# A mixed attention, recurrence and mixture-of-experts kernel: eight instead of six values units behind the recurrence, and the rotation's additions on GpSimd

## The reference, cut to what matters

```
h = rms_norm(x, g_mix);  proj = h @ w_in
q, k, v, q_idx, k_idx, w_idx = split(proj[dsa part])     # 8 heads of 128; 16 index heads of 64
r, d_w, kr, vr, d_a, d_g = split(proj[recurrent part])   # 16 heads of 64
q = rope(rms_norm(q) * q_gain);  k = rope(rms_norm(k) * k_gain)
q_idx = rope(q_idx);  k_idx = rope(k_idx)
rope(x) = [x1 * cos - x2 * sin, x2 * cos + x1 * sin]
iscore = sum over heads of relu(q_idx . k_idx) * w_idx   # the 64 best keys of each query are kept
y_dsa = softmax(q . k * scale, over the kept keys) @ v
y_rwkv = group_norm(recurrence(r, decay, k, v, ...)) ...
x = x + concat(y_dsa, y_rwkv) @ w_out                    # then experts, then the second block
```

## Time and profile before

| | us |
|---|---|
| median of the runs shown (three) | 3061.78 |
| lowest, highest | 3061.53, 3063.14 |
| the profiled execution's own time | 3059.96 |
| its span in the trace | 3058.2 |
| busy: PE, DVE, ACT, POOL | 2963.6, 1918.1, 1533.6, 162.1 |

### The profile page before, as it was taken

The page is one execution under the profiler, slowest core; times in us unless marked ns, Lnnn a source line. Parts: engine busy times, 40 slices in busy tenths (PEclk is TensorE's granted clock), DMA queues, the critical chain, the costliest instruction groups (busy, mean ns, idle before and its releaser), DMA issues.

```text
span 3058.2 us, 53182 instructions
## 1 busy us (share of the span) xinstructions
PE 2963.6 (97%) x22088; PEld 2645.5 (87%) x22088; DVE 1918.1 (63%) x2591; ACT 1533.6 (50%) x2132; POOL 162.1 (5%) x248
## 2 busy tenths in 40 slices
PE   8999999879899999999999999999999999999998
PEld 7888888768688887776999999999989989898996
DVE  6555555774677878877759954445665545455554
ACT  6445444454566666665543347654344434343443
POOL 0000000200000000000075400000000000000000
PEclk9999999989999999999999999999999999999999
DMA  6233233223588888886444444446555555555554
GB/s 235 85 110 111 98 111 103 89 88 124 191 319 332 321 335 318 329 318 260 152 166 154 152 165 165 167 178 218 182 193 193 193 187 186 192 182 190 191 182 150
DMA packets 81952, 582.43 MB, mean 190 GB/s; under 512 B 9024, under 2 KB 9280, under 8 KB 12480
## 3 DMA queue, kind: packets, MB, share of 16 engines
q1 hardware_dynamic: 79056, 566.45, 50.9%
q10 hardware_dynamic: 2672, 12.71, 1.1%
HBM read 574.93 MB, written 4.19 MB: 189 GB/s over the span
## 4 chain that ended last, share of the span: by engine, by line
PE 87%; DVE 9%; ACT 2%; issue 1%; DMA 0%; ACTq 0%; SPq 0%; DVEq 0%
PE PG L806 10%; PE PG L804 10%; PE PG L807 10%; PE PG L831 6%; PE PG L832 6%; PE PG L830 6%; PE PG L862 5%; PE PG L1241 4%; PE PG L1242 4%; PE PG L1243 4%; PE PG L863 3%; PE PG L864 3%; DVE ring_r L706 3%; PE PX L949 2%; PE PX L1293 1%
## 5 line engine op out<-in xcount | busy, mean ns | idle before, releaser
L706 DVE TENSOR_TENSOR ring_r<-ring,work_r 128x1024 fp32r<-128x1024 f32 x492 | 583.7, 1229 | 334.1 <-ACT work_r L699 330.6
L699 ACT ACTIVATE work_r<-ring 128x1024 fp32r<-128x1024 f32 x492 | 493.1, 1052 | 560.7 <-PE PG L807 290.4
L699 ACT ACTIVATE C_r<-ring 128x1024 fp32r<-128x1024 f32 x268 | 269.1, 1052 | 420.6 <-PE PG L807 296.6
L807 PE MATMUL PG<-YT_r,ring_r 128*128 128x256 f32 x1664 | 469.7, 282 | 0.0
L706 DVE TENSOR_TENSOR ring_r<-ring,C_r 128x1024 fp32r<-128x1024 f32 x268 | 319.7, 1234 | 218.3 <-ACT C_r L699 215.0
L807 PE MATMUL PG<-work_r,ring_r 128*128 128x256 f32 x1344 | 374.7, 279 | 0.0
L807 PEld LDWEIGHTS PG<-YT_r,ring_r 128*128 128x128 f32 x1664 | 316.3, 190 | 0.0
L864 PE MATMUL PG<-HT_r,ring_r 128*128 128x256 f32 x960 | 271.1, 282 | 0.0
L807 PEld LDWEIGHTS PG<-work_r,ring_r 128*128 128x128 f32 x1344 | 253.3, 188 | 0.0
L831 PE MATMUL PG<-ring_r,HT_r 128*128 128x512 f32 x624 | 246.6, 395 | 0.0
L804 PE MATMUL PG<-YT_r,C_r 128*128 128x256 f32 x832 | 238.4, 286 | 6.4 <-DVE ring_r L706 6.4
(11 more groups left out here) (649 smaller groups left out, 7138.4 us busy)
## 6 DMA issues: line engine op xcount, KB each, us to landing
ring<-weights SPq DMA_DIRECT2D x472, 1024.0 KB, 4.8
C<-weights SPq DMA_DIRECT2D x32, 1024.0 KB, 4.9
work<-weights SPq DMA_DIRECT2D x32, 1024.0 KB, 4.9
work<-xT SPq DMA_DIRECT2D x4, 512.0 KB, 7.0
XT<-x ACTq DMA_DIRECT2D x1, 2048.0 KB, 8.2
residual<-XT ACTq DMA_DIRECT2D x4, 512.0 KB, 3.0
XT<-residual ACTq DMA_DIRECT2D x1, 2048.0 KB, 12.3
result<-YT SPq DMA_DIRECT2D x8, 256.0 KB, 2.9
```

What stands on the lines that cost most here:

```text
L699: act.activation(w_high(u)[:, c], weights(u)[:, c], ACT.Copy).then_inc(w_hi, 1)
L706: dve.tensor_tensor(w_low(u)[:, c], weights(u)[:, c], w_high(u)[:, c].bitcast(F32), ALU.subtract).then_inc(w_lo, 1)
L807: last = pe.matmul(o, wl, high[:, k, :], start=False, stop=(n == kts - 1), skip_group_check=True)
```

## The change

Two more v tiles (25 and 26) are moved behind the recurrence: `LATE` is 8, the last pair fills with 4 units instead of 6. The late products are placed anew: ten before PE's wait for `out`, one per square, three per rotation step, 21 in the index steps. The wait for the last tile before the rotation (`DSA_TAKEN`) moves on PE behind the squares and on ACT becomes a wait per tile. ACT's and DVE's splits and ACT's `take_v` of the late units are placed anew. In the rotation, the addition of the two parts goes from DVE to POOL: DVE only writes the sine part (four buffers instead of two, signal a_sin), POOL makes the cosine part (two buffers instead of four) and adds. PE's step r waits for the sine part r - 2, no longer for the finished tile.

```diff
-LATE = 6
-DSA_PER_PAIR = [3] * 7 + [6]
+LATE = 8
+DSA_PER_PAIR = [3] * 7 + [4]
-FILL_UNITS = 6
+FILL_UNITS = [6] * 7 + [4]
...
-        ROPE_C, ROPE_S = cube(area(4 * T), 4), cube(area(2 * T), 2)
+        ROPE_C, ROPE_S = cube(area(2 * T), 2), cube(area(4 * T), 4)
...
             def attention():
+                values(0, 10)
                 pe.wait_ge(DR.sem, DR.at(MT - 1, "out"))
-                pe.wait_ge(free_bank(DSA_TAKEN), DSA_TAKEN // BANKS + 1)
                 for n in range(16):
                     ...
-                    values(n, n + 1)
-
+                    values(10 + n, 11 + n)
+
+                pe.wait_ge(free_bank(DSA_TAKEN), DSA_TAKEN // BANKS + 1)
                 for r in range(25):
                     if r >= 9:
                         pe.wait_ge(a_nrm, r - 8)
                     if r >= 2:
-                        pe.wait_ge(a_rope, r - 1)
+                        pe.wait_ge(a_sin, r - 1)
                     ...
-                    values(16 + 2 * r, 18 + 2 * r)
-
-                values(66, 68)
+                    values(26 + 3 * r, 29 + 3 * r)
+
+                values(101, 103)
                 pe.wait_ge(a_rope, 25)
                 ...
-                values(68, 72)
+                values(103, 107)
...
-                    if 72 + n < LATE * KT:
-                        values(72 + n, 73 + n)
+                    if 107 + n < LATE * KT:
+                        values(107 + n, 108 + n)
...  ACT
-                act.wait_ge(free_bank(DSA_TAKEN), DSA_TAKEN // BANKS + 1)
                 for n in range(16):
+                    if n in (1, 8):
+                        half_high(act, 2 * V_UNIT + 4 + n // 8)
+                    u = P1_AT["dsa", 9 + n]
+                    act.wait_ge(free_bank(u), u // BANKS + 1)
                     if n >= 4:
                         act.wait_ge(a_sum, n - 3)
                     act.activation(SQ[:, n % 4, :], DQ[:, 9 + n, :], ACT.Square).then_inc(a_sq, 1)
-                half_high(act, 2 * V_UNIT + 4)
-                half_high(act, 2 * V_UNIT + 5)
+                half_high(act, 2 * V_UNIT + 6)
                 ... (logarithm and exponential)
+                half_high(act, 2 * V_UNIT + 7)
                 take_v(0)
-                for q in range(1, 4):
-                    half_high(act, 2 * (V_UNIT + 2 + q))
-                    half_high(act, 2 * (V_UNIT + 2 + q) + 1)
+                take_v(1)
+                half_high(act, 2 * V_UNIT + 8)
+                for q in range(2, 6):
                     take_v(q)
+                    half_high(act, 2 * V_UNIT + 5 + 2 * q)
+                    if q < 5:
+                        half_high(act, 2 * V_UNIT + 6 + 2 * q)
...  DVE
+                    if n in (3, 10):
+                        half_low(dve, 2 * V_UNIT + 4 + n // 10)
...
-                late = dict(zip((2, 4, 11, 13, 18, 20), range(2 * V_UNIT + 4, HALVES)))
+                late = dict(zip((3, 6, 9, 11, 14, 16, 19, 22), range(2 * V_UNIT + 6, HALVES)))
                 for r in range(25):
                     if r in late:
                         half_low(dve, late[r])
                     if 9 <= r + 1 < 25:
                         normed(r + 1)
                     dve.wait_ge(a_rot, r + 1)
-                    link(dve.tensor_tensor(ROPE_S[:, r % 2, :], PX[:, 2 + r % 2, 0:T],
-                                           con("sin64" if r < 9 else "sin128"), ALU.mult))
-                    dve.wait_ge(a_cos, r + 1)
-                    dve.tensor_tensor(DQ[:, r, :], ROPE_S[:, r % 2, :], ROPE_C[:, r % 4, :], ALU.add) \
-                       .then_inc(a_rope, 1)
+                    if r >= 4:
+                        dve.wait_ge(a_rope, r - 3)
+                    dve.tensor_tensor(ROPE_S[:, r % 4, :], PX[:, 2 + r % 2, 0:T],
+                                      con("sin64" if r < 9 else "sin128"), ALU.mult).then_inc(a_sin, 1)
...  POOL
-            for r in range(25):
-                pool.wait_ge(a_sq, 1) if r < 9 else pool.wait_ge(a_nrm, r - 8)
-                if r >= 4:
-                    pool.wait_ge(a_rope, r - 3)
-                pool.tensor_tensor(ROPE_C[:, r % 4, :], DQ[:, r, :], con("cos64" if r < 9 else "cos128"),
-                                   ALU.mult).then_inc(a_cos, 1)
+            for n in range(26):
+                if n < 25:
+                    pool.wait_ge(a_sq, 1) if n < 9 else pool.wait_ge(a_nrm, n - 8)
+                    if n >= 2:
+                        pool.wait_ge(a_rope, n - 1)
+                    pool.tensor_tensor(ROPE_C[:, n % 2, :], DQ[:, n, :], con("cos64" if n < 9 else "cos128"),
+                                       ALU.mult).then_inc(a_cos, 1)
+                if n >= 1:
+                    r = n - 1
+                    pool.wait_ge(a_cos, r + 1)
+                    pool.wait_ge(a_sin, r + 1)
+                    pool.tensor_tensor(DQ[:, r, :], ROPE_S[:, r % 4, :], ROPE_C[:, r % 2, :], ALU.add) \
+                        .then_inc(a_rope, 1)
```

More of the change, by code:

```diff
@@ L318, in filling @@
                            for r, name in steps])
-        upto += [KT * FILL_UNITS * p + int(KT * FILL_UNITS * n) // int(share[-1]) for n in share]
-    halves = 2 * FILL_UNITS * MT
+        upto += [KT * sum(FILL_UNITS[:p]) + int(KT * FILL_UNITS[p] * n) // int(share[-1]) for n in share]
+    halves = 2 * sum(FILL_UNITS)
     return upto, [next(i for i, n in enumerate(upto) if n >= KT // 2 * (j + 1)) for j in range(halves)]
@@ L420, in build @@
         DR = Steps(sem("rwkv_dve"), DVE_RW)
-        a_sq, a_sum, a_ms, a_rs, a_nrm, a_rot, a_cos, a_rope = (sem("qk_" + n) for n in (
-            "squared", "summed", "mean_square", "inverse_root", "normed", "rotated", "cos_part", "roped"))
+        a_sq, a_sum, a_ms, a_rs, a_nrm, a_rot, a_sin, a_cos, a_rope = (sem("qk_" + n) for n in (
+            "squared", "summed", "mean_square", "inverse_root", "normed", "rotated", "sin_part", "cos_part", "roped"))
         a_vt, a_v, a_is, a_relu, a_acc, a_bias = (sem("idx_" + n) for n in (
@@ L1721, in attention @@
                     act.activation(RL[:, n % 4, 0:keys], PX[:, n % 4, 0:keys], ACT.Relu).then_inc(a_relu, 1)
-                    if n in (12, 31):
-                        take_v(4 + n // 31)
+                    if n in (8, 24):
+                        take_v(6 + n // 24)
                 act.dma_start(XTOK, A["x"]).then_inc(s_xtok, 16)
```

## The result

| us | before | after |
|---|---|---|
| median of one sitting, 18 executions each | 3061.66 | 3066.20 |
| lowest, highest | 3058.37, 3065.88 | 3061.24, 3078.44 |
| the profiled execution's own time | 3059.96 | 3075.25 |

The ratio after to before is 1.0024, 95% interval 1.0015 to 1.0033: slower by a quarter of a per cent. The forecast of 3065.9 is 0.3 us off, but that closeness is partly luck: the 18 times fall in two groups, eleven from 3061.24 to 3068.31 (median 3064.03) and seven from 3075.25 to 3078.44, and the median falls between. The profiled execution is of the upper group. The page's first line and the trace of the profiled execution of after, by stage: the joint, the squares, the rotation, the idle time before the transposes, the transposes, and the index scores (columns as in the earlier trace rows).

What follows compares the result with a forecast made beforehand. PE, busy 97% of the span, was taken to bound the kernel, DVE its rotation. Terms -10.1 + 0.5 + 1.7 + 1.0 + 11.3 + 1.7 - 2.0 gave +4.1 us, median 3065.9 us, range 3059 to 3072 (3052 to 3075 with rivals).

Steps and rivals of the forecast that it cites:

- A: Last recurrence pair: 28 fewer products ahead of the first group norm product, -10.1 us, with +0.5 for uncovered steps.
- B: End of the recurrence: half_low falls ahead of DVE's var and waits for ACT's half_high, +1.7 us.
- C: Sums of squares: waits at splits, with the half-clock stretch kept, +1.0 us; without that stretch -0.7.
- D: Rotation, 25 steps: bound by POOL, with collisions with DVE's two-SBUF-input instructions, 51.1 us against 39.8, +11.3 us.
- E: After the rotation: PE idles near 7 us for POOL's last adds, then half clock, +1.7 us (bounds 0 and +3.4).
- F: Index scores: 21 filled steps instead of 24, each 0.66 us cheaper unfilled, -2.0 us.
- Rival 1: Rotation: PE-bound at 39.7 us, splits falling into POOL's gaps, no E; total -9.0, 3052.8 us; chance 0.16.
- Rival 2: Rotation: DVE becomes the longer line and POOL waits for each sine; total +11.3, 3073.1 us; chance 0.16.
- Rival 3: Last recurrence pair: with less cover it runs at the pace of the chains; 3072 us; chance 0.08, shared with other.

Runs made afterwards that it cites:

- after_again: The changed kernel run once more without an edit; 3064.49 us, ratio 1.0019 to the kernel before, again in two groups.
- var_first: The changed kernel with DVE's half_low of the last recurrence pair kept behind var; 3066.09 us from five executions.
- psum_high: The changed kernel, ACT also copying the high half into PSUM for the rotation's eight splits, DVE subtracting from there; 3077.79 us, ratio 1.0037.
- refill: The changed kernel with nine late products moved from the index steps ahead of PE's wait for the last addition; 3063.38 us, ratio 1.0000.
- pool_best: The changed kernel with refill, var_first and step 6's half_high between ACT's logarithm and exponential; 3062.36 us, ratio 1.0001.

## Why the prediction was right or wrong

By stages, from the common zero, in us against before; the last row stands at the value transposes behind the index scores.

| | forecast | after | after_again |
|---|---|---|---|
| A, last pair | -9.6 | -9.5 | -9.5 |
| B, joint | +1.7 | +1.8 | +1.8 |
| C, squares | +1.0 | +0.5 | +1.8 |
| D, rotation | +11.3 | +9.9 | +9.9 |
| E, clock at the transposes | +1.7 | +1.7 | +1.7 |
| F, index stage | -2.0 | +13.9 | -0.2 |
| sum | +4.1 | +18.3 | +5.5 |

The spans differ from before's by 15.2 and 3.9. What the table leaves is -2.1 and +0.5 ahead of the zero, and -1.0 and -2.1 behind the last row, where half-clock stretches stand at other places in each execution. That wasn't followed.

**A and B** held to 0.1, B by its own mechanism (var_first takes it back). **C**: the slow stretch came again; it cost 0.5 in one profiled execution of the changed kernel (granted clock 0.90) and 1.8 in the other (0.82), around the +1.0 that was said. In var_first it did not come (1.00).

**D** is 1.4 too high, with the right mechanism. Its step was too small (1.58 measured, 1.50 said: a cosine product starts 0.14 after the end of the addition before it, where 0.08 had been read off), its collisions with norms too dear (0.18 each, 0.28 said, and at nine of the sixteen), the splits' a little (six POOL instructions of 1.71 to 1.73 and two of 1.53, +7.5 in all; 7.8 said), the stop at step 6 near (1.56, 1.7 said). These errors partly offset. Rival 1 (PE-bound, 39.7) fell: PE was busy 40.3 of 49.8. Rival 2 fell: DVE was busy 34.0, and POOL waited on it at step 6 (1.56) and once more for 0.48, and not again. Rival 3 fell with A. The Trainium skill, GPSIMD Engine Reference, section 1 (Specifications), names the two-SBUF-input contention, and this case's runs agree with it in both directions: 1.73 us with two SBUF inputs, 0.74 with one in PSUM (psum_high). The Trainium skill, Trainium Architecture — The Big Picture, "What this means for kernel authors", calls it an exclusive lock and not a split of bandwidth; the 1.73, which is 0.73 and most of a split's 1.22, agrees.

**E** is the term that failed, not in its mechanism but in its length. Its idle time, said to be near 7 us, was 5.36. It said 3.4 us at half clock behind it, from the one example in the earlier trace rows. In the lower group it is little more: the granted clock is down for 4.7 us of work in after_again (602.16 to 606.9), and from the transposes to the first index product it takes 4.15 us (602.16 to 606.31) where before took 2.43 (597.58 to 600.01), +1.7. In the upper group's profile the stretch held on for over 40 us, and the index stage, first product to value transposes, took 42.9 us where after_again took 28.8. The bounds of 0 and +3.4 should have been 0 and about +16. One example of a stretch is no bound on its length.

**F** failed in its mechanism. It took the index stage for PE's; the end of the stage is DVE's. Before, then after_again:

```profile
621.70 0.23 DVE L2319 TENSOR_SCALAR work<-work 128x128 f32<-128x128 f32 x1
621.85 0.35 DVE L2307 TENSOR_SCALAR work<-work 128x256 f32<-128x256 f32 x1
622.23 3.62 DVE L2309 SCALAR_TENSOR_TENSOR work<-work 128x256 f32<-128x256 f32 x7
626.04 4.13 DVE L2309 SCALAR_TENSOR_TENSOR work<-work 128x256 f32<-128x256 f32 x8 [0.19 <-ACT work L1721]
```

```profile
628.34 0.23 DVE L2327 TENSOR_SCALAR work<-work 128x128 f32<-128x128 f32 x1
628.48 0.35 DVE L2315 TENSOR_SCALAR work<-work 128x256 f32<-128x256 f32 x1
628.87 7.78 DVE L2317 SCALAR_TENSOR_TENSOR work<-work 128x256 f32<-128x256 f32 x15
```

DVE first finishes the search of the first 128 rows (its last instructions are those at 621.70 and 628.34). Then it makes one product (0.35) and fifteen sums of 0.52 in a row, and waits only once, for ACT's relu (0.19). PE's filled steps 17 to 24 stand beside that search, and the three that the change leaves empty are among them. From the first index product to the last sum it is 30.2 us before (600.01 to 630.17) and 30.3 after_again (606.31 to 636.65), three filled steps fewer or not. In refill, which empties four of the first sixteen steps too, the stage did get shorter (25.9), so a filled step is free only beside the search. In the upper group PE does bound the stage: its filled steps take 2.08 us at half clock (629.00 to 631.08), and DVE waits up to 1.60 us for them. The earlier trace rows showed PE's step of 1.18 and DVE's of 0.50 at different times; who ends the stage could have been read there.

So the total was right by errors that offset each other. D 1.4 too dear stands against F 1.8 too generous; C, E and the rest behind the table vary by a microsecond or two between executions. The lower group lies at +2.4 (3064.03 against 3061.66) where +4.1 was said, and the upper group, which no term foresaw, lifts the median to +4.5. That the median met the forecast to 0.3 us is luck; that the change costs a little, by a rotation bound by POOL, is not.

## What to carry to other kernels

Work moved into another engine's free time has to be priced with that engine's neighbours running: an addition of 0.74 us on POOL took 1.73 beside a long instruction on DVE with two SBUF inputs, and that instruction took 1.42 to 1.67 instead of 1.22. Idle time on PE is not to be booked at its own length alone: what followed the same 5.4 us of waiting cost another 1.5 us by the end of the index scores in one profiled execution and 15.6 in the other, and the two groups of times lie 12 us apart (medians 3064.03 and 3076.20). And a stage's length is to be read on the engine whose last instruction releases the next stage, not on the one whose rows are the longest.

## What the runs showed of the hardware

Behind the same 5.36 us without a matmul, the granted clock stood at 0.50 for 5 us of work in one execution and for over 40 in another of the same kernel. The matmuls in it (16 before the index scores, 116 and more in them) left no gap in the long case: PE was busy for 39.10 of 39.10 us at half speed, where it is busy 27.11 of 28.80 in after_again, which is at full clock for nearly all of the stage. None of the 31 executions without an idle time before the transposes is in an upper group or has a mean clock of 0.985 or less, and 26 of the 68 with 2.71 us or more are and have. It isn't a simple function of the length, since 2.71 (psum_high) did so in seven of ten and 3.39 in one of eleven. With 2.16 us the one profile (refill) has half clock for 3.3 us behind it (600.8 to 604.1) and the other (pool_best) none, and where the low clock of four of those 20 executions lies, no profile shows. What decides within one kernel stays open.

A POOL instruction that meets DVE's 1024-element subtraction is delayed by up to 1.0 us of that subtraction's 1.22 (1.73 for 0.73); one that meets a norm multiplication by 0.18 (0.92 for 0.74); and with one operand of the subtraction in PSUM the delay is nil.
